# A routed-expert loop turned from two blocks per turn to one, with one set of rooms, in a hybrid decoder layer

## The chip, the cores and the metric

The kernel runs on one core of one Trainium2 chip. A core has TensorE (PE; its weight loads are listed apart as PEld), VectorE (DVE), ScalarE (ACT), GpSimd (POOL) and SyncE (SP), and 16 DMA engines that the queues of SP, ACT and POOL share. The metric is the device time of one execution in microseconds (us), of which the median of several runs is taken.

## The reference, cut to what matters

The program is one layer of a decoder trunk (2048 tokens, width 1024): a mixer (retention, Mamba-2 and S5 side by side), cross-attention, a hierarchical mixture of experts, and a last RMSNorm. The change touches the experts and the last norm only.

```python
def hier_moe(xn, w_rg, b_rg, w_re, b_re, w_gate, w_up, w_down):
    ...                                   # top-1 of 4 groups, then top-2 of its 8 experts
    flat_e = expert.reshape(-1)           # 4096 pairs (token, expert)
    counts = jnp.bincount(flat_e, length=N_EXPERTS)
    padded = (counts + MOE_BLOCK - 1) // MOE_BLOCK * MOE_BLOCK     # blocks of 128 rows
    ...
    def expert_block(args):
        xb, e = args
        h = jax.nn.silu(xb @ w_gate[e]) * (xb @ w_up[e])           # 1024 -> 512
        return h @ w_down[e]                                       # 512 -> 1024
    ...
    y = ybuf[dest].astype(F32) * sw[:, None]
    return jax.ops.segment_sum(y, st, num_segments=T).astype(xn.dtype)
```

Each expert's rows are filled up to whole blocks of 128. When the pairs that the reference routes on its own inputs are counted, all 32 experts get rows: 17 of them between 79 and 127 (one block each) and 15 between 133 and 203 (two blocks each). That makes 47 blocks, 6016 rows, of which 1920 are padding. In order of the experts the numbers of blocks are 2 1 1 2 2 2 2 2 1 2 2 1 2 1 1 2 1 1 1 2 1 1 2 2 1 1 2 1 1 1 2 1.

## The kernel before, in words

`experts` (line 2007) first routes on DVE with some help of PE, and writes a plan: for each block its expert, and whether it is the first block of its expert. Then all engines walk over the blocks. `finish` is the last norm.

**Number format.** Each f32 operand is split in two f16 halves, the nearest value and the rest, and a product is three f16 matmuls (`products`, line 110). So the weights of an expert (gate, up and down, 2 MB each) come in six pieces of 1 MB into six rooms `w_rows`; ACT takes the nearest (`nearest`, L2197), DVE the rest (`rest`, L2419), into one of two slots of `wg`, `wu` and `wd`, of which the current expert uses one and the next the other. A room is loaded again when DVE has taken its rest. The split of expert u+1 is tied to the first block b of expert u (`following`): gate and up pieces in step b, down pieces in step b+1.

**A step b** is, on PE: gate products of block b (24 matmuls), `turn_h(b-1)` (transposes of the hidden rows of b-1), `turn_x(b+1)` (transposes of the tokens of b+1, L2506), up products of b (24), down products of b-1 (24). ACT and DVE split the transposed tokens (`take_x`, L2224, and `x_rest`, L2437, into `xT`), apply silu (L2219) and product (L2432), split the hidden rows (`take_h`, `h_rest`), and ACT takes the result `y` out (`take_y`, L2234). Gate products of a block wait for its tokens and for the first two pieces of its expert; up products for the other two.

**Order of ACT and DVE in a step b.** ACT: down pieces (if any), silu(b), take_h(b-1), take_x(b+1), gate and up pieces (if any), take_y(b-1). DVE: down rests, h_rest(b-1), x_rest(b+1), gate and up rests, product(b).

**POOL** gathers the 128 token rows of a block from `xn_scr` into `xr` (L2143, an indirect DMA of 512 KB) and adds the 128 rows of `y` into `ybuf` (L2150, an indirect DMA that accumulates). Every room `xr`, `xT`, `sg`, `hT`, `y` is there twice, and a turn of the loop has two blocks, written out. So a gather waits for the transposes of two blocks earlier, and in POOL's list the adds stand two turns behind the gathers. The number of turns is rounded up: the loop runs 48 blocks, the last of them padding alone. Padding rows are moved like others: they gather row 2047, and they are added to 128 spare rows behind `ybuf`.

**finish** loads 16 chunks of 512 KB (SP), squares on ACT, mean on DVE, power on POOL, scaling on DVE, and stores each chunk (SP).

Of the kernel before, what the change touches and what calls it, by code (L numbers as in the profile page):

```python
# [17 lines left out]
F32 = mybir.dt.float32  # L18
F16 = mybir.dt.float16
I32 = mybir.dt.int32  # L20
U32 = mybir.dt.uint32
# [4 lines left out]
P = 128  # L26
# [1966 lines left out]
HB = 2  # L1993
# [3 lines left out]
MAX_TURNS = NB // HB - 1  # L1997
MIN_TURNS = (USED_MIN - 1) // HB

# [4 lines left out]
LISTED = 18  # L2004


def experts(nc, env, dram, logits, cst):
# [4 lines left out]
    with ExitStack() as ctx:  # L2012
# [18 lines left out]
        spare = [wd[:, 1, :, :, :].rearrange("p h k n -> p (h k n)").bitcast(F32), y[0][:, :], y[1][:, :]]  # L2031
# [29 lines left out]
        rows_from, rows_to = sb("rows_from", [P, NB], U32), sb("rows_to", [P, NB], U32)  # L2061
# [7 lines left out]
        x_ld = [sem(f"rows_gathered{i}") for i in range(HB)]  # L2069
# [3 lines left out]
        y_st = [sem(f"y_added{i}") for i in range(HB)]  # L2073
        NT = NB // HB
# [61 lines left out]
        @block.gpsimd  # L2136
        def _(pool):
            pool.wait_ge(rows_ok, 2)
# [6 lines left out]
            def add(b):  # L2145
# [4 lines left out]
                pool.indirect_dma_start(dram["ybuf"], bass.IndirectOffsetOnAxis(ap=rows_to[:, b:b + 1], axis=0), y[b % HB][:, :], None,  # L2150
                                        compute_op=ALU.add).then_inc(y_st[b % HB], 16)

            LATE = 2
            gather(0)
            gather(1)
            pool.wait_ge(planned, 1)
            used = turns_used(pool)
            for t in range(1, NT + LATE):
                if t < USED_MIN // HB:
                    gather(HB * t)  # L2160
                    gather(HB * t + 1)
                elif t < NT:
                    with pool.If(used + 1 > t):
                        gather(HB * t)
                        gather(HB * t + 1)
                if LATE <= t < USED_MIN // HB + LATE:
                    add(HB * (t - LATE))
                    add(HB * (t - LATE) + 1)
                elif t >= LATE:
                    with pool.If(used + 1 > t - LATE):  # L2170
                        add(HB * (t - LATE))
                        add(HB * (t - LATE) + 1)
            for i in range(HB):
                pool.wait_ge(y_st[i], used * 16 + 16)

        def steps(eng, first, step, last):
# [4 lines left out]
            with eng.Fori(0, MAX_TURNS) as t, eng.If(t < used):  # L2181
                step(t * HB + 1, 1, t)
                step(t * HB + 2, 0, t + 1)
            last(used * HB + 1, used)

        @block.scalar
        def _(act):
# [29 lines left out]
            def silu(b, i):  # L2217
                act.wait_ge(gd, b + 1)
                act.activation(sg[i][:, :], bank[2][:, :], ACT.Silu, scale=1.0 / (W_SCALE * X_SCALE)).then_inc(sil, 1)  # L2219

            def take_x(b, i):
# [470 lines left out]
```

## Time and profile before

| what | value |
|---|---|
| median of 3 runs (2547.68 to 2552.76) | 2551.65 us |
| the profiled execution itself | 2546.03 us |
| its span, first to last instruction | 2544.2 us |
| mean granted clock of PE | 0.959 |
| busy: PE, DVE, ACT, POOL | 2303.1, 1400.8, 983.4, 331.0 us |
| experts, first token transposes to last down product | 1633.1 to 2484.1 us |
| finish, first load to last landing | 2496.6 to 2544.2 us |

The span is cut in stages one after another. The mixer and cross-attention take the first 1590 us, routing some 40 us, the expert loop 850 us and `finish` 48 us. In a timeline a row is a run of equal instructions of one engine: start, length, engine, line, operation, output<-inputs, count, and in brackets the idle time before it with what ended that. Matmul rows overlap their successor by about 0.16 us, since the end of a matmul is modelled; the distance between two starts is the better measure.

### The profile page before, as it was taken

How to read it: one execution, taken by the hardware profiler on the slowest of the kernel's cores; microseconds unless marked ns; L12 is line 12 of the kernel's file. 1: busy time of each engine (PE TensorE's matmuls, PEld its weight loads, DVE VectorE, ACT ScalarE, POOL GpSimd, SP SyncE). 2: the span in 40 equal slices, each digit the busy share in tenths (PEclk: the TensorE clock that was granted, in tenths of full speed). 3: DMA queues.
4: the chain of work that ended last, by engine and by line, in shares of the span. 5: the costliest groups of instructions: out<-in, count | busy, mean ns of one | idle time of the engine just before them, and what ended most of it. 6: DMA issues, size and time to landing. Idle time of an engine off the chain costs nothing. (4 is left out here: it accounts for less than half of the span.)

```text
span 2544.2 us, 34574 instructions
## 1 busy us (share of the span) xinstructions
PE 2303.1 (91%) x12015; PEld 1304.5 (51%) x12016; DVE 1400.8 (55%) x2030; ACT 983.4 (39%) x1423; POOL 331.0 (13%) x275
## 2 busy tenths in 40 slices
PE   4999999999959988999999998489999999999980
PEld 2465565655648963555555554245545454444440
DVE  5566565565649843333333332867556578757823
ACT  4522533323221332222221221346545567646723
POOL 0022121210230000000000000012122221212112
PEclk8999999999979999999999999599999999999995
DMA  5201001001050142111111001579779899999927
GB/s 190 87 26 58 1 25 59 1 26 44 9 207 34 42 180 88 40 67 42 59 67 67 25 34 50 190 254 339 250 244 322 267 351 348 325 308 340 337 66 288
DMA packets 151077, 366.25 MB, mean 144 GB/s; under 512 B 24512, under 2 KB 30016, under 8 KB 150720
## 3 DMA queue, kind: packets, MB, share of 16 engines
q1 hardware_dynamic: 137152, 314.52, 33.8%
q0 software_dynamic: 13824, 50.34, 8.2%
q8 instruction: 69, 1.13, 0.2%
q14 instruction: 32, 0.26, 0.0%
HBM read 303.48 MB, written 61.34 MB: 143 GB/s over the span
## 5 line engine op out<-in xcount | busy, mean ns | idle before, releaser
L110 PE MATMUL bankA<-main_room,hnT 128*128 128x512 f16 (+1 forms) x1536 | 301.6, 354 | 5.5 <-DVE main_room L569 5.5
L110 PE MATMUL bankE<-wg,xT 128*128 128x512 f16 x1152 | 261.5, 384 | 20.9 <-DVE xT L2437 16.8
L110 PE MATMUL bankE<-wd,hT 128*128 128x512 f16 x1152 | 256.5, 379 | 1.7 <-DVE hT L2442 1.7
L110 PE MATMUL bankE<-wu,xT 128*128 128x512 f16 x1152 | 256.6, 379 | 0.0
L110 PEld LDWEIGHTS bankA<-main_room,hnT 128*128 128x128 f16 x1536 | 151.1, 99 | 147.7 <-issue 6.8
L110 PEld LDWEIGHTS bankE<-wg,xT 128*128 128x128 f16 x1152 | 113.8, 99 | 160.9 <-issue 28.8
L110 PEld LDWEIGHTS bankE<-wd,hT 128*128 128x128 f16 x1152 | 112.6, 98 | 137.6 <-issue 1.9
L110 PE MATMUL bankA<-hnT,main_room 128*128 128x512 f16 x768 | 174.2, 390 | 8.9 <-DVE hnT L545 8.9
L110 PEld LDWEIGHTS bankE<-wu,xT 128*128 128x128 f16 x1152 | 112.8, 98 | 125.5 <-issue 0.2
L110 PE MATMUL bankC<-w_probs,probsT 128*128 128x512 f16 x768 | 172.4, 382 | 0.0
L110 PE MATMUL bankC<-main_room,hnT_c 128*128 128x512 f16 x768 | 170.7, 379 | 0.0
L2419 DVE SCALAR_TENSOR_TENSOR wg<-w_rows,wg 128x2048 f16<-128x2048 f32 x64 | 143.9, 2287 | 31.7 <-ACT wg L2197 29.8
L2419 DVE SCALAR_TENSOR_TENSOR wd<-w_rows,wd 128x2048 f16<-128x2048 f32 x64 | 144.3, 2288 | 25.1 <-ACT wd L2197 25.0
L2419 DVE SCALAR_TENSOR_TENSOR wu<-w_rows,wu 128x2048 f16<-128x2048 f32 x64 | 144.3, 2286 | 14.1 <-ACT wu L2197 14.1
L2143 POOL DMA_INDIRECT xr<-scratch_xn_scr,rows_from x48 | 81.8, 1704 | 479.0 <-PE bankE L2506 435.4
L2197 ACT ACTIVATE wd<-w_rows 128x2048 f16<-128x2048 f32 x64 | 120.0, 1906 | 39.4 <-issue 24.5
L2442 DVE SCALAR_TENSOR_TENSOR hT<-bankE,hT 128x512 f16<-128x512 f32 x48 | 33.0, 687 | 184.0 <-ACT hT L2228 184.0
L110 PE MATMUL bankC<-w_out_s,catT 128*128 128x512 f16 x576 | 129.6, 379 | 1.4 <-DVE w_probs L1826 1.4
L2197 ACT ACTIVATE wu<-w_rows 128x2048 f16<-128x2048 f32 x64 | 119.5, 1899 | 26.1 <-DMA w_rows<-in_w_up 26.1
L110 PEld LDWEIGHTS bankA<-hnT,main_room 128*128 128x128 f16 x768 | 76.3, 100 | 103.9 <-issue 19.3
L2197 ACT ACTIVATE wg<-w_rows 128x2048 f16<-128x2048 f32 x64 | 119.1, 1904 | 25.8 <-issue 19.6
L1686 POOL TENSOR_TENSOR rs_c<-ms_c,nhalf_c 128x1 f32<-128x1 f32 x32 | 17.4, 543 | 827.2 <-DVE ms_c L1789 827.2
(365 smaller groups left out, 3389.6 us busy)
## 6 DMA issues: line engine op xcount, KB each, us to landing
w_rows<-in_w_gate SPq DMA_DIRECT2D x64, 1024.0 KB
w_rows<-in_w_up SPq DMA_DIRECT2D x64, 1024.0 KB
w_rows<-in_w_down SPq DMA_DIRECT2D x64, 1024.0 KB
x_room<-in_x SPq DMA_DIRECT2D x4, 2048.0 KB, 10.9
cat_t<-scratch_cat SPq DMA_DIRECT2D x16, 512.0 KB, 4.8
main_room<-in_x SPq DMA_DIRECT2D x16, 512.0 KB, 5.5
scratch_ybuf<-main_room SPq DMA_DIRECT2D x16, 512.0 KB, 2.6
hf<-scratch_ybuf SPq DMA_DIRECT2D x16, 512.0 KB, 12.0
```

What stands on the lines that cost most here:

```text
L110: ins = pe.matmul(o, a[x][k], b[y][k], start=start and k == 0 and j == 0, stop=stop and k == n - 1 and j == 2)
L1686: pool.tensor_tensor(rs[:, k, c:c + 1], ms[:, k, c:c + 1], nhalf[:, 0:1], ALU.pow).then_inc(rsd, 1)
L2143: pool.indirect_dma_start(xr[b % HB][:, :], None, dram["xn_scr"], bass.IndirectOffsetOnAxis(ap=rows_from[:, b:b + 1], axis=0)).then_inc(x_ ...
L2197: act.activation(place(p, slot, 0), room(p), ACT.Copy, scale=W_SCALE).then_inc(done, 1)
L2419: dve.scalar_tensor_tensor(place(p, slot, 1), room(p), W_SCALE, place(p, slot, 0), ALU.mult, ALU.subtract).then_inc(done, 1)
L2442: dve.scalar_tensor_tensor(hT[i][:, 1, :, :], bank[4][:, :].rearrange("p (k n) -> p k n", k=FT), H_SCALE, hT[i][:, 0, :, :], ALU.mult, ALU ...
```

## The change

- The loop has one block per turn and one room each of `xr`, `xT`, `sg`, `hT` and `y`. The number of turns is the number of blocks less two: 47 blocks are run.
- `turn_x(b+1)` on PE stands behind the up products of b.
- ACT: take_h(b-1), silu(b), down pieces, take_x(b+1), gate and up pieces, take_y(b-1). DVE: h_rest(b-1), down rests, product(b), x_rest(b+1), gate and up rests.
- POOL alternates: gather(b+1), which waits for the transposes of block b, then add(b-1), which waits for the add before it and for `y`. take_y(b) waits for the add of b-1 to have landed. The last block's add uses a list of its own, `rows_end`.
- Gather and add carry a bound of T-1 on the row number, and rows beyond it (the padding) are left out. `xr` is cleared once by DVE at the start of routing.
- Before the loop, DVE takes x_rest(1) ahead of the gate and up rests of expert 1.
- `finish` issues its even chunk loads on SP and its odd ones on ACT.

```diff
-MAX_TURNS = NB // HB - 1
-MIN_TURNS = (USED_MIN - 1) // HB
+MAX_TURNS = NB - 3
+MIN_TURNS = USED_MIN - 2
...
-        xr = [sb(f"xr{i}", [P, D]) for i in range(HB)]
-        xT = [sb(f"xT{i}", [P, 2, KT, P], F16) for i in range(HB)]
-        sg = [sb(f"sg{i}", [P, DE]) for i in range(HB)]
-        hT = [sb(f"hT{i}", [P, 2, FT, P], F16) for i in range(HB)]
-        y = [sb(f"y{i}", [P, D]) for i in range(HB)]
+        xr, xT = sb("xr", [P, D]), sb("xT", [P, 2, KT, P], F16)
+        sg, hT, y = sb("sg", [P, DE]), sb("hT", [P, 2, FT, P], F16), sb("y", [P, D])
...
             def gather(b):
-                if b >= HB:
-                    pool.wait_ge(xt, 2 * (b - HB) + 2)
-                pool.indirect_dma_start(xr[b % HB][:, :], None, dram["xn_scr"], bass.IndirectOffsetOnAxis(ap=rows_from[:, b:b + 1], axis=0)).then_inc(x_ld[b % HB], 16)
...
                 if b:
-                    pool.wait_ge(y_st[(b - 1) % HB], (b - 1) // HB * 16 + 16)
+                    pool.wait_ge(xt, 2 * b)
+                pool.indirect_dma_start(xr[:, :], None, dram["xn_scr"], bass.IndirectOffsetOnAxis(ap=rows_from[:, b:b + 1], axis=0),
+                                        bounds_check=T - 1, oob_is_err=False).then_inc(x_ld, 16)
+
+            def add(b, rows):
+
+                if b:
+                    pool.wait_ge(y_st, b * 16)
                 pool.wait_ge(y_t, b * 2 + 2)
...
+            def turn(b):
+                gather(b + 1)
+                add(b - 1, rows_to[:, b - 1:b])
...
         @block.scalar
...
-            def step(b, i, k):
+            def step(b):
+                take_h(b - 1)
+                silu(b)
                 following(act, b - 1, downs_(b - 1))
-                silu(b, i)
-                take_h(b - 1, 1 - i)
-                take_x(b + 1, 1 - i)
+                take_x(b + 1)
                 following(act, b, gates_ups(b))
-                take_y(b - 1, 1 - i, k if i else k - 1)
+                take_y(b - 1)
...
         @block.vector
...
+            dve.memset(xr[:, :], 0.0).then_inc(x_clear, 1)
...
             def first():
...
-                product(0, 0)
+                product(0)
+                x_rest(1)
                 gate_up_rest(1, 1)
-                x_rest(1, 1)
...
-            def step(b, i, k):
+            def step(b):
+                h_rest(b - 1)
                 following(dve, b - 1, down_rest)
-                h_rest(b - 1, 1 - i)
-                x_rest(b + 1, 1 - i)
+                product(b)
+                x_rest(b + 1)
                 following(dve, b, gate_up_rest)
-                product(b, i)
...
         @block.tensor
...
-            def step(b, i, k):
-                def turns():
-                    turn_h(b - 1, 1 - i)
-                    turn_x(b + 1, 1 - i, k + 1 if i else k)
-
-                by_slot(b, gate_up(b, i, turns))
-                by_slot(b - 1, down(b - 1, 1 - i))
+            def step(b):
+                by_slot(b, gate_up(b, lambda: turn_h(b - 1)))
+                turn_x(b + 1)
+                by_slot(b - 1, down(b - 1))
...
         @block.scalar
         def _(act):
+            for c in range(1, NCH, 2):
+                act.dma_start(H[c][:, :], hv[c]).then_inc(h_ld[c], 16)
```

PE, one step of the loop as it stood before: `wg`, `wu` and `wd` are gate, up and down weights, `cst_all,xr` the token transposes, `cst_all,sg` those of the hidden rows.

```order
L110 MATMUL bankE<-wg,xT 128x512 x24
L2514 MATMUL bankE<-cst_all,sg 128x128 x4
L2500 ISA
L2501 ISA
L2506 MATMUL bankE<-cst_all,xr 128x128 x8
L2538 REGISTER_ALU
L110 MATMUL bankE<-wu,xT 128x512 x24
...
L110 MATMUL bankE<-wd,hT 128x512 x24
```

The same step now.

```order
L110 MATMUL bankE<-wg,xT 128x512 x24
L2514 MATMUL bankE<-cst_all,sg 128x128 x4
L2538 REGISTER_ALU
L110 MATMUL bankE<-wu,xT 128x512 x24
...
L2500 ISA
L2501 REGISTER_ALU
L2506 MATMUL bankE<-cst_all,xr 128x128 x8
...
L110 MATMUL bankE<-wd,hT 128x512 x24
```

The token transposes moved from ahead of the up products to behind them; between them and the next gate products only the down products stand.

POOL, from the first gathers into the loop, before.

```order
L2143 DMA xr<-scratch_xn_scr,rows_from 128x1024 x2
L2079 TENSOR_LOAD plan
L2079 ISA x2
L2143 DMA xr<-scratch_xn_scr,rows_from 128x1024 x4
L2150 DMA scratch_ybuf<-y,rows_to 2176x1024 x2
L2143 DMA xr<-scratch_xn_scr,rows_from 128x1024 x2
```

And now.

```order
L2141 DMA xr<-scratch_xn_scr,rows_from 128x1024 x2
L2076 TENSOR_LOAD plan
L2076 ISA x2
L2141 DMA xr<-scratch_xn_scr,rows_from 128x1024
L2149 DMA scratch_ybuf<-y,rows_to 2176x1024
L2141 DMA xr<-scratch_xn_scr,rows_from 128x1024
```

Six gathers stood ahead of the first add; now three do, and the add of block b-2 stands directly ahead of the gather of block b+1.

## Rows read from the trace of the kernel before

**Rows 1.** Page, part 1: busy us (share of the span) and instructions.

```profile
PE 2303.1 (91%) x12015; PEld 1304.5 (51%) x12016; DVE 1400.8 (55%) x2030; ACT 983.4 (39%) x1423; POOL 331.0 (13%) x275
```

**Rows 2.** Windows of the loop: busy us (instructions), then clock, DMA share, GB/s.

```profile
core 0: us, PE busy (x) PEld busy (x) DVE busy (x) ACT busy (x) POOL busy (x), PEclk, DMA share, GB/s
1680.00:2450.00 770.00, 762.43 (x3790) 379.05 (x3789) 516.33 (x361) 472.25 (x450) 154.25 (x88) 1.00 0.89 297
```

**Rows 3.** Page, part 5: the gate matmuls; idle before them and its releaser.

```profile
L110 PE MATMUL bankE<-wg,xT 128*128 128x512 f16 x1152 | 261.5, 384 | 20.9 <-DVE xT L2437 16.8
```

**Rows 4.** Timeline, PE, from the token transposes in the step of a one-block expert.

```profile
2062.55 1.04 PE L2506 MATMUL bankE<-cst_all,xr 128*128 128x128 f32 x8
2063.42 5.34 PE L110 MATMUL bankE<-wu,xT 128*128 128x512 f16 x24
2068.60 5.34 PE L110 MATMUL bankE<-wd,hT 128*128 128x512 f16 x24
```

**Rows 5.** Timeline, DVE, same step: rests of tokens, then of gate weights.

```profile
2065.41 1.28 DVE L2437 SCALAR_TENSOR_TENSOR xT<-bankE,xT 128x512 f16<-128x512 f32 x2
2067.23 4.50 DVE L2419 SCALAR_TENSOR_TENSOR wg<-w_rows,wg 128x2048 f16<-128x2048 f32 x2 [0.53 <-issue]
```

**Rows 6.** Timeline, ACT: take_x of that step; gate pieces and take_y in another.

```profile
2063.29 1.09 ACT L2224 ACTIVATE xT<-bankE 128x512 f16<-128x512 f32 x2
...
2098.73 3.71 ACT L2197 ACTIVATE wg<-w_rows 128x2048 f16<-128x2048 f32 x2 [0.65 <-issue]
...
2105.95 0.57 ACT L2234 ACTIVATE y<-bankE 128x512 f32<-128x512 f32 x1
2107.68 0.60 ACT L2234 ACTIVATE y<-bankE 128x512 f32<-128x512 f32 x1 [1.16 <-PE bankE L110]
```

**Rows 7.** Timeline, POOL: the add that follows that take_y.

```profile
2109.05 1.98 POOL L2150 DMA_INDIRECT scratch_ybuf<-y,rows_to  x1 [8.60 <-ACT y L2234]
```

**Rows 8.** One line's instructions (ns min/median/max): gathers of the loop, one of them, adds.

```profile
L2143 POOL DMA_INDIRECT xr<-scratch_xn_scr,rows_from x43: 939/1879/2650, 1693.2 to 2408.1; - x43
...
DMA to landing us min/median/max: 4.1/8.4/10.1
...
L2143 POOL DMA_INDIRECT xr<-scratch_xn_scr,rows_from x1: 1522/1522/1522, 2080.7 to 2080.7; - x1
...
DMA to landing us min/median/max: 7.9/7.9/7.9
...
L2150 POOL DMA_INDIRECT scratch_ybuf<-y,rows_to x42: 1582/1616/2621, 1694.4 to 2386.2; - x42
...
DMA to landing us min/median/max: 6.0/9.5/11.3
```

**Rows 9.** Timeline, PE: four instructions behind an idle stretch of PE.

```profile
2166.30 1.12 PE L2514 MATMUL bankE<-cst_all,sg 128*128 128x128 f32 x4 [2.93 <-DVE sg L2432]
2167.21 1.91 PE L2506 MATMUL bankE<-cst_all,xr 128*128 128x128 f32 x8
...
2425.92 0.66 PE L2514 MATMUL bankE<-cst_all,sg 128*128 128x128 f32 x4 [2.51 <-DVE sg L2432]
...
2458.82 7.03 PE L110 MATMUL bankE<-wg,xT 128*128 128x512 f16 x24 [4.15 <-issue]
```

**Rows 10.** Waits of PE, 1680 us to the end: total us, times, longest.

```profile
PE bankE L2514 <- DVE sg L2432: 7.5, 4, 2.9
```

**Rows 11.** Timeline, start of the loop: product(0), x_rest(1), gate products of block 1.

```profile
1656.97 0.75 DVE L2432 SCALAR_TENSOR_TENSOR sg<-bankE,gate_of,sg 128x512 f32<-128x512 f32 x1
...
1666.45 1.28 DVE L2437 SCALAR_TENSOR_TENSOR xT<-bankE,xT 128x512 f16<-128x512 f32 x2
...
1668.08 6.65 PE L110 MATMUL bankE<-wg,xT 128*128 128x512 f16 x24 [12.57 <-DVE xT L2437]
```

**Rows 12.** Timeline, DVE: a clearing of 512 columns at the start of routing.

```profile
1593.48 0.48 DVE L2268 MEMSET wd<- 128x512 f32 x1 [0.46 <-PEq L1565]
```

**Rows 13.** Windows of finish, columns as in rows 2.

```profile
2522.00:2532.00 10.00, 0.00 (x0) 0.00 (x0) 7.99 (x12) 2.90 (x6) 5.58 (x5) 0.50 1.03 419
```

More of the change, by code:

```diff
@@ L1992 @@
 WHOLE = 12582912.0
-HB = 2
 SLOTS = 2
@@ L2068, in experts @@
         hi_gu, lo_gu, hi_dn, lo_dn = sem("gate_up_nearest"), sem("gate_up_rest"), sem("down_nearest"), sem("down_rest")
-        x_ld = [sem(f"rows_gathered{i}") for i in range(HB)]
+        x_ld = sem("rows_gathered")
         lists, marked, listed, rows_ok = sem("list_steps"), sem("pairs_marked"), sem("rows_listed"), sem("rows_known")
@@ L2072, in experts @@
             "xT_done", "xT_nearest", "xT_rest", "gate_done", "up_done", "silu_done_e", "h_ready", "hT_done", "hT_nearest", "hT_rest", "down_done", "y_taken"))
-        y_st = [sem(f"y_added{i}") for i in range(HB)]
-        NT = NB // HB
+        y_st, y_end, end_st = sem("y_added"), sem("last_y_taken"), sem("last_y_added")
+        x_clear = sem("rows_cleared")
         block = ctx.enter_context(nc.Block())
@@ L2157, in _ @@
             used = turns_used(pool)
[L2158 to L2174, printed above, removed]
+            def turn(b):
+                gather(b + 1)
+                add(b - 1, rows_to[:, b - 1:b])
+            for b in range(1, MAX_TURNS + 2):
+                if b < USED_MIN:
+                    turn(b)
+                else:
+                    with pool.If(used + 2 > b):
+                        turn(b)
+            pool.wait_ge(lists, LISTED)
+            pool.wait_ge(y_end, 2)
+            pool.indirect_dma_start(dram["ybuf"], bass.IndirectOffsetOnAxis(ap=rows_end[:, :], axis=0), y[:, :], None,
+                                    bounds_check=T - 1, oob_is_err=False, compute_op=ALU.add).then_inc(end_st, 16)
+            pool.wait_ge(end_st, 16)
+            pool.wait_ge(x_ld, used * 16 + 48)
         def steps(eng, first, step, last):
@@ L2181, in steps @@
             with eng.Fori(0, MAX_TURNS) as t, eng.If(t < used):
-                step(t * HB + 1, 1, t)
-                step(t * HB + 2, 0, t + 1)
-            last(used * HB + 1, used)
+                step(t + 1)
+            last(used + 1)
         @block.scalar
@@ L2238, in first, with last @@
                     nearest(p, 0, 0)
-                take_x(0, 0)
-                silu(0, 0)
+                take_x(0)
+                silu(0)
                 for p in GU:
                     nearest(p, 1, 1)
-                take_x(1, 1)
-            def step(b, i, k):
+                take_x(1)
+            def step(b):
+                take_h(b - 1)
+                silu(b)
                 following(act, b - 1, downs_(b - 1))
-                silu(b, i)
-                take_h(b - 1, 1 - i)
-                take_x(b + 1, 1 - i)
+                take_x(b + 1)
                 following(act, b, gates_ups(b))
-                take_y(b - 1, 1 - i, k if i else k - 1)
-            def last(b, k):
+                take_y(b - 1)
+            def last(b):
+                take_h(b - 1)
+                silu(b)
                 following(act, b - 1, downs_(b - 1))
-                silu(b, 1)
-                take_h(b - 1, 0)
-                take_y(b - 1, 0, k)
-                take_h(b, 1)
-                take_y(b, 1, k)
+                take_y(b - 1)
+                take_h(b)
+                take_y(b, y_end)
             steps(act, first, step, last)
@@ L2446, in first @@
                     rest(p, 0, 0)
-                x_rest(0, 0)
+                x_rest(0)
                 for p in GU[2:]:
@@ L2528, in rows @@
                         return [[w[:, slot, h, kt, :] for kt in range(KT)] for h in range(2)]
-                    tokens = [[xT[i][:, h, kt, :] for kt in range(KT)] for h in range(2)]
+                    tokens = [[xT[:, h, kt, :] for kt in range(KT)] for h in range(2)]
                     pe.wait_ge(x_hi, b * 2 + 2)
@@ L2541, in gate_up, with down @@
                 return products_of
-            def down(b, i):
+            def down(b):
                 def products_of(slot, u):
@@ L2596, in _ @@
         def _(sp):
-            hv = dram["ybuf"][0:T, :].rearrange("(c p) d -> c p d", p=P)
             ov = dram["out"][0].rearrange("(c p) d -> c p d", p=P)
-            for c in range(NCH):
+            for c in range(0, NCH, 2):
                 sp.dma_start(H[c][:, :], hv[c]).then_inc(h_ld[c], 16)
```

95 lines of the change are left out of this document (49 added, 46 removed).

## The prediction

> **What bounds the kernel now.** I read the busy shares first, then windows of the loop, then timelines of single steps. PE is busy for 91% of the span [rows 1], and in the loop for 762.4 of 770 us at full clock [rows 2]: nothing but PE sets the pace there, although the DMA engines are 89% busy beside it. So a step costs what its PE work costs. By the starts in [rows 4] that is 0.87 us for the token transposes (2062.55 to 2063.42) and 5.18 us for 24 products (2063.42 to 2068.60), three times in a step; the four hidden transposes take half of the eight, 0.43. The step is 0.87 + 0.43 + 3 x 5.18 = 16.84 us. Of the gate products' 20.9 us of idle time 16.8 are waits for split tokens, all ahead of the loop [rows 3]. The question is thus not what engines save, but whether PE still finds its operands ready.
>
> **What the change takes away.**
> (a) Block 48. The blocks of the reference are 47, and 48 are run (1152 gate matmuls [rows 3] / 24). One step less: -16.8 us. Its weights are those of the last expert, so no load goes with it.
> (b) Block 1's tokens. x_rest(1) began at 1666.45, behind four gate and up rests, though product(0) had ended at 1657.7 [rows 11]. Now it follows product(0): 8.7 us earlier, and PE has nothing else to wait for: -8.7 us. The rests behind it then end where x_rest(1) used to, in time for block 2.
> (c) In four steps PE waited 7.5 us in all for product(b) [rows 10], which stood behind rests of late weights. It now stands ahead of the rests. I take -5.
> (d) Routing: clearing 1024 columns is twice the 0.48 us of [rows 12], and four small steps ahead of the gate list less two steps of the turn count add some 0.4: +1.4 us.
> (e) Padding rows: 1920 of 6016 are not moved. Where PE is the bound, this is worth nothing by itself; it can only shorten the waits below.
> (f) finish: in its middle the DMA engines run at a share of 1.03 and 419 GB/s [rows 13]. Its 17 MB in and out set its length, and a second issuing queue moves no byte faster: 0, between -2 (an earlier start of the first loads) and +4 (eight issues on ACT ahead of its first square).
> Together -29 us.
>
> **What it adds: a wait for weights.** I count from the start of turn_x. Tokens must be turned, split, and then, where block b is the only one of its expert, the gate pieces of the next expert must be split before PE can begin gate(b+1). In [rows 4, 5] this chain took from 2062.55 to 2067.23 + 4.50 = 2071.73, that is 9.18 us, and hid below up and down products (11.2 us with the transposes). The chain keeps its order on ACT and DVE; product(b) is slipped in while take_x runs and costs nothing. But turn_x now has only the down products behind it: 0.87 + 5.18 = 6.05 us of cover. PE waits 9.18 - 6.05 = 3.13 us. If the expert before had one block too, two down rests (4.5) stand ahead on DVE in the same step: hidden transposes end 5.6 us into the step, take_h, silu and the plan's loads bring the first down piece to 7.2, its nearest takes 1.9 (3.71 for two, [rows 6]), two rests end at 13.6, product and x_rest at 15.6, and with 0.5 of issue and 4.5 the gate rests at 20.6: 3.75 us late against 16.84. Of the 17 one-block experts 16 have a successor, 8 of them behind another one-block expert: 8 x 3.13 + 8 x 3.75 = **+55 us**. In a two-block expert's second step, x_rest ends at 15.6 by the same count, 1.2 before it is due, and nothing waits.
>
> **What it adds: a wait for the gather.** gather(b+1) used to be two blocks ahead; the adds behind it could be late. Now it stands behind add(b-2), which stands behind take_y(b-2), which stands behind the four pieces on ACT in a step b-1 that splits. From the start of gate(b-1): turn_x starts at 10.8; take_x ends 1.83 later (2062.55 to 2064.38, [rows 4, 6]), 12.6; the plan 0.7; four pieces 7.2 (2098.73 to 2105.95, [rows 6]), 20.5; take_y 1.1, 21.6; add after 0.8 (2108.28 to 2109.05, [rows 6, 7]), its 1.6 to 2.0 us of issue [rows 7, 8] and a gap of 0.3: the gather starts at 24.4. PE wants the rows for turn_x(b+1) at 16.84 + 10.8 = 27.6. With L from issue to landing it waits L - 3.2. L was 4.1 to 10.1, median 8.4 [rows 8]; none of these gathers had to hurry. What the trace doesn't show is a gather directly behind an add, with four weight loads just issued. The floor is 4.1, the ceiling 10.1. I take 7.9, the row of 2080.7 [rows 8], a gather issued while weight loads were still draining as here: 4.7 us, for 14 two-block experts (the first one's split lies ahead of the loop): +65 us (floor 13, ceiling 97). For one-block experts PE is 3.1 to 3.75 late already and the wait is L - 6.6, 1.3 us; a slower clock (next) delays the need as well, so I count half, 0.6 x 16 = +10 (floor 0, ceiling 50). **+75 us** in all.
> The landing of one gather is also priced by the Trainium skill ("DMA: Bandwidth & Descriptors", section "Anatomy of one DMA — SWDGE (gpsimd) path"): about 2.0 us + bytes / 436e3, which for 512 KB is 3.2 us. By it no two-block step would wait, and the sum would be 65 us less. [Rows 8] disagree: 4.1 at best, 8.4 in the median, beside weight loads.
> The skill also says, against this change, to double-buffer so that DMA overlaps compute ("Trainium Kernel Development and Optimization", section "Best Practices"); the trace of before has only the doubled rooms.
>
> **What it adds: clock.** Behind an idle stretch of 2.93 us the hidden and token transposes took 1.12 and 1.91 us, against 0.66 behind one of 2.51 us [rows 9] and 1.04 in the loop [rows 4]: they ran at the lower level of the clock, some 1.3 us lost. Behind 4.15 us, 24 products took 7.03 [rows 9] against 5.34 [rows 4]: 1.7 lost. The 30 waits above are 3.1 to 4.7 us long, on this edge. Between 0 and 1.7 each; I take 1.0: **+30 us**.
>
> **Sum.** Against the profiled execution's own 2546.0 us (span 2544.2 and 1.8 around it): 2546 - 29 + 55 + 75 + 30 = 2677. The timed median stands 5.6 us above that execution. I forecast **2678 us**, about 5% more.
>
> **Rivals.**
> *The gather comes at its unloaded speed* (L = 4.1). For it: missing padding rows and longer steps relieve the DMA engines. Against: four loads of 1 MB are issued 17 to 24 us into the very step. Then 55 + 13 + clock on 16 waits, 16: 2546 - 29 + 84 = 2601.
> *The gather waits for the add's rows* (L = 10.1 or more, clock lost at every wait). For it: both go through one queue, and adds need 9.5 us in the median [rows 8]. 2546 - 29 + 55 + 97 + 38 + 50 = 2757.
> *Not slower.* The waits for weights don't come, because the gate rests are done within the 6.05 us behind turn_x; then only (a) to (d) remain, 2517. This needs rests that start 1.5 us after turn_x does; in [rows 4, 5] they started after 4.7. It decides at 3.1 us per step, and I see no row for it.
> *The turn count isn't what it says.* If 48 blocks still ran, each case is 17 us longer. The count of the reference speaks against it.
>
> **Chances.** Forecast 0.68 (its own range 2630 to 2725), unloaded gather 0.16, queued gather 0.11, not slower 0.04, the last 0.01. The range 2608 to 2742 leaves about 2 in 10 outside. A measurement tells about 0.2% (5 us) from no change: faster 0.04, same 0.01, slower 0.95.
>
> **What would show each step.** In the changed profile: 1128 gate matmuls; the gate products' idle time near 55 us in 16 or so waits of 3 to 4 us for DVE `wg`; the token transposes idle near 75 us for the DMA of `xr`; gate products of block 1 at about 1660; PE near 85% busy in the loop; transposes of 1.1 or products of 7 us behind some waits; finish still 48 us long. Wrong it would be if PE's wait for `xr` were near zero or above 100 us, which is the choice of L, or if one-block steps took 16.8 us.

## The result: 9% slower, 1.75 times what was forecast

The changed kernel takes 2772.6 us (median of 4 runs, 2770.6 to 2774.8), the kernel before 2550.7 beside it: a ratio of 1.087, 95% interval 1.085 to 1.089, or +222 us. The forecast was 2678 us, +127; its own sum of terms is +131. The direction was as forecast, and so were the two kinds of wait; the size was not, the empty turns of the loop were missing from the sum, and the time lies outside the range.

The profiled execution has a span of 2773.0 us against 2544.2. Page, part 1, of the changed kernel, and its window of the loop (columns as in [rows 2]):

```profile
PE 2360.8 (85%) x11931; PEld 1318.9 (48%) x11932; DVE 1405.2 (51%) x2029; ACT 986.1 (36%) x1417; POOL 334.7 (12%) x274
```

```profile
1680.00:2450.00 770.00, 632.61 (x2874) 304.34 (x2872) 389.50 (x271) 358.29 (x338) 124.04 (x68) 0.90 0.65 214
```

PE, busy for 762.4 of these 770 us before [rows 2], is now busy for 632.6, at a mean clock of 0.90, and the DMA engines' share fell from 0.89 to 0.65. They are less loaded and yet they are what PE waits for. The waits of PE from 1600 us to the end of the changed kernel (what PE waited for, then total us, times, longest):

```profile
PE bankE L2506 <- DMA xr<-scratch_xn_scr,rows_from: 139.4, 31, 9.0
PE bankE L110 <- DVE wg L2419: 37.5, 16, 3.0
...
PE bankE L110 <- issue: 14.3, 10, 10.2
...
PE bankE L110 <- DVE wd L2419: 1.3, 4, 0.6
```

Page, part 5, the groups of PE that take these waits (the first answers to [rows 3]):

```profile
L110 PE MATMUL bankE<-wg,xT 128*128 128x512 f16 x1128 | 274.1, 403 | 54.7 <-DVE wg L2419 37.5
...
L110 PE MATMUL bankE<-wd,hT 128*128 128x512 f16 x1128 | 283.2, 413 | 7.1 <-issue 4.1
...
L2506 PE MATMUL bankE<-cst_all,xr 128*128 128x128 f32 x376 | 64.8, 330 | 139.4 <-DMA xr<-scratch_xn_scr,rows_from 139.4
```

The instructions behind waits also ran longer. Timeline of PE in the changed kernel, three places where transposes or gate products waited:

```profile
1701.59 5.35 PE L110 MATMUL bankE<-wg,xT 128*128 128x512 f16 x24 [2.99 <-DVE wg L2419]
...
2005.86 1.94 PE L2506 MATMUL bankE<-cst_all,xr 128*128 128x128 f32 x8 [9.00 <-DMA xr<-scratch_xn_scr,rows_from]
2007.60 6.94 PE L110 MATMUL bankE<-wd,hT 128*128 128x512 f16 x24
...
2092.89 1.06 PE L2506 MATMUL bankE<-cst_all,xr 128*128 128x128 f32 x8 [1.33 <-DMA xr<-scratch_xn_scr,rows_from]
2094.49 5.35 PE L110 MATMUL bankE<-wd,hT 128*128 128x512 f16 x24 [0.54 <-issue]
```

Behind 1.33 us of idleness nothing is lost, nor behind the 2.99 at 1701.59. Behind 9.00 us the transposes take 1.94 us, not 1.04, and the down products 6.94, not 5.34 [rows 4]: 2.5 us on top of the wait. The mean granted clock from 2006 to 2012 us is 0.60 of full speed, so part of that stretch ran at the lower level, 1.2 GHz.

The loop's own balance, from the start of block 1's gate products to the end of the last down products: 816.0 us before (1668.08 to 2484.08), 1051.4 now (1663.47 to 2714.86), although there is one step less. What stands in the 228.8 us by which the spans differ:

| where | us |
|---|---|
| one step less (counted, 16.84 us of work) | -16.8 |
| block 1's gate products, counted from the first token transposes | -8.8 |
| waits for the product (7.5 us before, none now) | -7.5 |
| finish, 47.6 to 45.3 us | -2.3 |
| first token transposes at 1637.35, not 1633.13; 2.4 of it arose ahead of routing | +4.2 |
| waits for `xr` in the loop, two-block experts' second steps (14 waits) | +93.3 |
| the same in the other steps (16 waits) | +45.2 |
| waits for `wg` | +37.5 |
| waits with no releaser in the profile, 14.3 against 4.15 [rows 9] | +10.1 |
| waits for the rests of `wd` | +1.3 |
| slow clock: gate, down and transpose groups longer than before per instruction, 18.1 + 32.1 + 14.3 | +64.5 |
| left over; 47 waits, each seen 0.16 us too short by the modelled ends of matmuls, would be 7.5 | +8.1 |

### The profile page after: what moved, and what is told of

It is laid out like the page before. It is cut to its first block and busy times, and to the rows that moved or that the text cites. A ratio compares the mean times of both kernels' runs of the same rounds, so it can differ in the third digit from the quotient of the medians.

```text
span 2773.0 us, 34998 instructions
## 1 busy us (share of the span) xinstructions
PE 2360.8 (85%) x11931; PEld 1318.9 (48%) x11932; DVE 1405.2 (51%) x2029; ACT 986.1 (36%) x1417; POOL 334.7 (12%) x274
## 5 line engine op out<-in xcount | busy, mean ns | idle before, releaser
L110 PE MATMUL bankE<-wg,xT 128*128 128x512 f16 x1128 | 274.1, 403 | 54.7 <-DVE wg L2419 37.5
L110 PE MATMUL bankE<-wd,hT 128*128 128x512 f16 x1128 | 283.2, 413 | 7.1 <-issue 4.1
L2149 POOL DMA_INDIRECT scratch_ybuf<-y,rows_to x46 | 119.2, 2590 | 869.4 <-ACT y L2231 829.1
L2506 PE MATMUL bankE<-cst_all,xr 128*128 128x128 f32 x376 | 64.8, 330 | 139.4 <-DMA xr<-scratch_xn_scr,rows_from 139.4
L2419 DVE SCALAR_TENSOR_TENSOR wd<-w_rows,wd 128x2048 f16<-128x2048 f32 x64 | 143.8, 2288 | 65.6 <-ACT wd L2194 65.5
L2419 DVE SCALAR_TENSOR_TENSOR wg<-w_rows,wg 128x2048 f16<-128x2048 f32 x64 | 143.8, 2288 | 55.6 <-ACT wg L2194 55.6
L2419 DVE SCALAR_TENSOR_TENSOR wu<-w_rows,wu 128x2048 f16<-128x2048 f32 x64 | 143.6, 2285 | 0.0
L2221 ACT ACTIVATE xT<-bankE 128x512 f16<-128x512 f32 x94 | 53.1, 596 | 249.6 <-PE bankE L2506 249.6
L2194 ACT ACTIVATE wg<-w_rows 128x2048 f16<-128x2048 f32 x64 | 118.9, 1904 | 26.8 <-issue 26.6
L2506 PEld LDWEIGHTS bankE<-cst_all,xr 128*128 128x128 f32 x376 | 53.8, 171 | 156.4 <-issue 152.4
## 6 DMA issues: line engine op xcount, KB each, us to landing
w_rows<-in_w_up SPq DMA_DIRECT2D x64, 1024.0 KB, 10.4
```

The lines of the kernel that those rows point to most:

```text
L110: ins = pe.matmul(o, a[x][k], b[y][k], start=start and k == 0 and j == 0, stop=stop and k == n - 1 and j == 2)
L2194: act.activation(place(p, slot, 0), room(p), ACT.Copy, scale=W_SCALE).then_inc(done, 1)
L2221: act.activation(xT[:, 0, 4 * j:4 * j + 4, :], bank[j][:, :].rearrange("p (k n) -> p k n", k=4), ACT.Copy, scale=X_SCALE).then_inc(x_hi, 1)
L2419: dve.scalar_tensor_tensor(place(p, slot, 1), room(p), W_SCALE, place(p, slot, 0), ALU.mult, ALU.subtract).then_inc(done, 1)
L2506: ins = pe.transpose(bank[j][:, n * P:(n + 1) * P], xr[:, kt * P:(kt + 1) * P], ident[:, :])
```

## The experiments

Seven of them change the changed kernel (e...), seven the kernel before (b...). All times are medians; where a kernel ran more than once, a ratio to the kernel before with its 95% interval is given. `...` marks lines left out of an edit.

**e1: the place of the gather in POOL's list.** The changed kernel, with the gather of b+1 ahead of the add of b-2.

```diff
-                gather(b + 1)
-                add(b - 1, rows_to[:, b - 1:b])
...
+                gather(b + 1)
+                if b > 1:
+                    add(b - 2, rows_to[:, b - 2:b - 1])
```

> The changed kernel with one thing moved in POOL's list: gather(b+1) stands ahead of add(b-2) instead of behind it. Rooms, order on PE, ACT and DVE, and padding stay. Theory A (the place in the list is what makes the gather late; one room is enough): the gather is issued right behind the transposes of block b, some 16 us before its rows are wanted, and even at 9 us to landing it is in time. PE's wait for xr (139.4 us in the changed kernel) falls under 10, the slow-clock stretches behind it go too (some 45 us), and the time falls from 2773 to about 2590. Rival B (the one room itself is what costs): the wait stays above 60 us, since the room is free only after the transposes of the block before, and the time stays above 2680.

Measured: 2578.2 us (one run), 194 us less. Its waits of PE:

```profile
PE bankE L110 <- DVE wg L2420: 49.0, 16, 3.4
...
PE bankE L2507 <- DMA xr<-scratch_xn_scr,rows_from: 0.9, 1, 0.9
```

The waits for `xr` in the loop are gone (the 0.9 us lie ahead of it), and with them most of the slow clock: the groups of PE are 11.7 us longer than before, not 64.5. The one room is kept. The room is not what costs; the add ahead of the gather is. The gather could start when the transposes have emptied `xr`, but it stands behind an add that stands behind take_y. The one room `y` has a wait too, since take_y needs the add before it to have landed (ACT waits 48.0 us for that here, in 13 places), but no wait of PE follows from it in this profile. Timeline of POOL in the changed kernel, and behind it in this one:

```profile
1774.60 1.59 POOL L2149 DMA_INDIRECT scratch_ybuf<-y,rows_to  x1 [18.17 <-ACT y L2231]
1776.49 1.04 POOL L2141 DMA_INDIRECT xr<-scratch_xn_scr,rows_from  x1 [0.30 <-issue]
1795.36 3.16 POOL L2149 DMA_INDIRECT scratch_ybuf<-y,rows_to  x1 [17.83 <-ACT y L2231]
1798.83 1.04 POOL L2141 DMA_INDIRECT xr<-scratch_xn_scr,rows_from  x1 [0.30 <-issue]
```

```profile
1732.48 2.13 POOL L2141 DMA_INDIRECT xr<-scratch_xn_scr,rows_from  x1 [11.74 <-PE bankE L2507]
1742.54 3.27 POOL L2149 DMA_INDIRECT scratch_ybuf<-y,rows_to  x1 [7.94 <-ACT y L2232]
```

**e2, e3, e7: what makes the landing slow.** In the changed kernel the adds lose all rows but row 0 (e2: bound 0 instead of T-1), the loop's weight loads bring a quarter of their bytes (e3), or both (e7). All three leave out work that the result needs, and are read for their time alone.

```diff
-                                        bounds_check=T - 1, oob_is_err=False, compute_op=ALU.add).then_inc(y_st, 16)
+                                        bounds_check=0, oob_is_err=False, compute_op=ALU.add).then_inc(y_st, 16)
...
+                    a = a // 2
+                    sp.dma_start(room(p)[:, 0:a, 0:256], rows[e].squeeze(0)[:, k:k + a, 0:256]).then_inc(w_ld[p], 16)
```

> The changed kernel, but the adds in the loop carry a bound of 0 on the row number, so that they leave out all rows but row 0: this leaves the experts' part out of the result, and the time is read for that. The adds stand where they stood and are issued as before. Theory C (the gather lands late because the add's 128 rows are ahead of it in the same queue): issue to landing of the gather, 7.9 us in the median and near 9 behind the four weight pieces, falls to 4 to 5, PE's wait for xr falls from 139 to 50 us or less, time about 2660. Rival D (weight loads in flight make it late): landing stays at 8 to 9 and the wait above 110 us; time within 20 us of 2773.

> The changed kernel, but in the loop each weight load brings a quarter of its bytes (half the rows of the piece, half the columns), the rest of the room stays what the first loads left; the result is wrong for that, and all splits and products run as before. Rival D: with a quarter of the weight traffic the gather behind an add lands in 4 to 6 us, and PE's wait for xr falls from 139 to about 60 us; time about 2670. Theory C: the add is still ahead of the gather, landing stays above 7.5 and the wait above 100 us.

> The changed kernel with both aids at once: the adds find no row within their bound (the experts' part of the output is left out) and the loop's weight loads bring a quarter of the bytes (later experts use stale weights). One alone took 43 and 77 us from the 139 us of waits for xr. If what is left is the gather's own late issue behind the add, it still waits where the landing takes longer than the 1.8 to 3.2 us that it has: a landing of 4.1 us, the fastest of the kernel before, would leave 14 to 31 waits of 1 to 2 us, 15 to 50 us in all, and about 2640 to 2670 us. If rows and loads were the whole cause, the waits are 0 to 19 us (139 less 43 less 77), and the time 2600 to 2640.

Measured: 2712.7, 2689.5 and 2653.8 us (one run each). The waits of PE for `xr`, in e2, e3 and e7 in turn:

```profile
PE bankE L2506 <- DMA xr<-scratch_xn_scr,rows_from: 97.6, 29, 6.4
```

```profile
PE bankE L2510 <- DMA xr<-scratch_xn_scr,rows_from: 62.3, 17, 6.2
```

```profile
PE bankE L2510 <- DMA xr<-scratch_xn_scr,rows_from: 46.4, 15, 5.3
```

The median from issue to landing of a gather was 7.9 us in the changed kernel, 6.6 in e2, 5.5 in e3 and, in e7 (DMA issues of its window from 1600 us on):

```profile
xr<-scratch_xn_scr,rows_from POOLq DMA_INDIRECT x48, 4.3
```

Taking away the adds' rows alone takes 42 us off the waits, the weight loads alone 77, both together 93. Neither is the whole cause, and for the adds' rows I had expected about twice as much. The last 46 us, 2.5 to 5.3 in each of 13 two-block experts and some 1 at two other places, are there although the landing has little left to contend with, a quarter of the weight bytes: that is the late issue itself. It is the rival of the unloaded gather (L = 4.1) with the issue where it really was.

**e4: the padding rows, in the changed kernel.** Bounds are taken off gather and add, so that padding is moved as in the kernel before.

```diff
-                                        bounds_check=T - 1, oob_is_err=False).then_inc(x_ld, 16)
...
-                                        bounds_check=T - 1, oob_is_err=False, compute_op=ALU.add).then_inc(y_st, 16)
+                                        compute_op=ALU.add).then_inc(y_st, 16)
```

> The changed kernel with its padding rows moved again as before (no bound on the row numbers; padding gathers row 2047 and is added behind the result). If leaving out padding shortened gathers and adds, this is slower: by theory C by 10 to 40 us, since the blocks before a late gather are often half empty and their add is short; if each of the 16 DMA engines has full lists either way, or landing is set by weight loads (rival D), it is the same within 10 us.

Measured: 2805.1 us (one run), 32 more; waits for `xr` 166.0 instead of 139.4 us, gathers landing after 9.5 us in the median instead of 7.9. Leaving padding out is worth 32 us here, 26.6 of them in these waits: a landing is what PE waits for here.

**b5: the padding rows, in the kernel before.** The same bounds, and both rooms `xr` cleared at the start of routing.

```diff
+            for room_x in xr:
+                dve.memset(room_x[:, :], 0.0).then_inc(x_clear, 1)
...
+                                        bounds_check=T - 1, oob_is_err=False).then_inc(x_ld[b % HB], 16)
```

> The kernel before with one edit: gathers and adds leave padding rows out (and both token rooms are cleared at the start of routing, 2 us of DVE). In the changed kernel leaving them out was worth 32 us, 26 of them in waits for a late gather. Here a gather is two blocks ahead and no wait for it is in the trace; if the saving lives only by that wait, it is 0 here, with a further -0 to -7 from the waits for a late product that stands behind late weights, and +2 for the clearing: 2549 us, between 2544 and 2553. If freed DMA time were worth something in itself, the time would be well below 2544.

Measured: 2542.2 us, ratio 0.9965 (0.9953 to 0.9977): -9.5 us, more of a gain than I expected. Its trace shows two places. Waits for the product are 2.9 us in one, against 7.5 in four [rows 10]. And the last block, which is padding alone, adds nothing: from the issue of the last add to the first load of finish it takes 8.0 us (2488.97 to 2496.98), before 11.1 (2485.46 to 2496.60). These are 7.7 us; the clearing costs some 2 of them back. PE's waits for the first tokens' rests are 15.4 us instead of 16.8, and I have no row for the rest.

**e5: the gate pieces ahead of the tokens.** e1, and on ACT and DVE the two gate pieces of the next expert are split ahead of take_x and x_rest, so that gate(b+1) would not wait for them. The part on DVE, against e1:

```diff
-                product(b)
+                following(dve, b, gate_rest)
+                product(b)
                 x_rest(b + 1)
-                following(dve, b, gate_up_rest)
+                following(dve, b, up_rest)
```

> e1_gather_first with the split of the gate pieces moved ahead of the tokens on ACT and DVE (the up pieces stay behind them). Theory E (the 49 us that PE still waits for the rest of wg are the chain turn_x, take_x, gate pieces behind the up products): where the expert before had two blocks, the gate rests now end 13.6 us into the step and x_rest at 15.6, in time for 16.84, so 8 of the 16 waits vanish. Where it had one, DVE has two down rests and two gate rests first (to 18.3) and x_rest ends near 20: 3.5 us of wait for xT instead of wg, 8 times. Sum: waits 49 to about 28 us, time 2578 to about 2540. Rival F (the wait is set by DVE's sum of work, whatever its order): waits stay at 49, time within 10 us of 2578.

Measured: 2615.9 us, ratio 1.026 (1.024 to 1.028): not 38 us faster than e1 but 38 slower. The wait changed its name. Timeline of DVE, and of PE, in e5:

```profile
1725.93 4.50 DVE L2426 SCALAR_TENSOR_TENSOR wd<-w_rows,wd 128x2048 f16<-128x2048 f32 x2 [2.19 <-ACT wd L2195]
1730.34 4.49 DVE L2426 SCALAR_TENSOR_TENSOR wg<-w_rows,wg 128x2048 f16<-128x2048 f32 x2
1734.74 0.75 DVE L2447 SCALAR_TENSOR_TENSOR sg<-bankE,gate_of,sg 128x512 f32<-128x512 f32 x1
1735.40 1.28 DVE L2452 SCALAR_TENSOR_TENSOR xT<-bankE,xT 128x512 f16<-128x512 f32 x2
```

```profile
1737.03 8.25 PE L110 MATMUL bankE<-wg,xT 128*128 128x512 f16 x24 [3.42 <-DVE xT L2452]
```

PE now waits for `xT`, 73.1 us in 32 places from 1600 us on, where e1 waits 49.0 for `wg`; 7.0 us in two of these places lie ahead of the loop and are in e1 too. The other half of the loss is the clock: the gate products take 287.0 us in all, in e1 268.6. This place had no wait in e1: its step is the first of a two-block expert, where the gate pieces aren't urgent and the tokens are. An order written once for all steps moves a wait from the steps that need the one to those that need the other.

**e6, b6: the empty turns.** The loop had a fixed number of turns and an `If` around each; here it has only those that are used, in e1 (e6) and in the kernel before (b6).

```diff
-            with eng.Fori(0, MAX_TURNS) as t, eng.If(t < used):
+            with eng.Fori(0, used) as t:
```

> e1_gather_first with a loop that runs as many turns as there are, instead of 61 of which the last 16 do nothing. Theory G (PE's 10.2 us idle ahead of the last block's gate products, 4.2 in the kernel before with 8 empty turns of 31, are the empty turns, 0.5 to 0.7 us each): the wait shrinks to 1 us or less and the time falls by 9 to 11 us, to about 2568. Rival H (it is the loading of the code of the last step): the wait stays near 10 and the time at 2578.

> The kernel before with a loop of as many turns as there are, instead of 31 of which the last 8 do nothing. Theory G: PE's wait of 4.2 us ahead of block 48 and the 1.7 us of slow clock behind it vanish, time 2550.5 falls by 4 to 6 us. Rival H: no change (within 2 us).

Measured: e6 2567.8 us, ratio 1.0072 (1.0054 to 1.009), 10.4 less than the one run of e1; b6 2544.1 us, ratio 0.9974 (0.9964 to 0.9984), 6.9 less than before, a little more than the 4 to 6 expected. The wait ahead of the last block's gate products, 10.24 us in the changed kernel and 4.15 before [rows 9], is gone in both. In the changed kernel, and in e6:

```profile
2689.16 7.46 PE L110 MATMUL bankE<-wg,xT 128*128 128x512 f16 x24 [10.24 <-issue]
```

```profile
2486.53 5.34 PE L110 MATMUL bankE<-wg,xT 128*128 128x512 f16 x24
```

The kernel before has 31 turns at most and uses 23, the changed one 61 and 45. So 8 empty turns cost 4.15 us and 16 cost 10.24, 0.52 and 0.64 each, and then the clock. The rival, the loading of the last step's code, falls with that: the code is the same and the wait is gone.

**b1, b2: two of the parts alone, in the kernel before.** x_rest(1) ahead of the gate and up rests; and 47 blocks, with a last step written out for an odd number. The edit of b1, and the heart of that of b2:

```diff
                 product(0, 0)
+                x_rest(1, 1)
                 gate_up_rest(1, 1)
-                x_rest(1, 1)
```

```diff
-            last(used * HB + 1, used)
+            odd = odd_count(eng)
+            with eng.If(odd > 0):
...
+                step(less * HB + 1, 1, less)
+                last(less * HB + 2, 0, less + 1)
+            with eng.If(odd < 1):
+                last(used * HB + 1, 1, used)
```

> The kernel before with one edit: DVE takes the rests of block 1's tokens ahead of the gate and up rests of expert 1. By the count from the rows the gate products of block 1 start 8.7 us earlier and everything behind them too: 2542.0 us, between 2540 and 2544. A rival: the rests of gate and up weights end 2.5 us later and with them the first product of the loop, so that block 2 waits and part of the gain is given back, 2545 or more.

> The kernel before, with 47 blocks run instead of 48: two blocks per turn and two sets of rooms as before, and behind the loop one step more and an ending of the other parity where the number of blocks is odd. Nothing else is changed. Theory I (a block is 16.84 us of PE work and nothing hides it): time 2550.5 falls by 15 to 18 us, to about 2534. Rival: the end of the loop is set by the adds or the code of the ending, and the gain is under 8 us.

Measured: b1 2543.4 us, ratio 0.9969 (0.9958 to 0.9979), -8.4; b2 2536.6 us, ratio 0.9942 (0.9926 to 0.9959), -14.5, just under the 15 to 18 expected. In b2 the written-out step brings one wait of its own:

```profile
PE bankE L110 <- DVE wu L2434: 5.8, 1, 5.8
```

**b8, b9: the late token transposes alone.** The kernel before, with two rooms, and turn_x behind the up products (b8); in b9 DVE also takes the product ahead of the tokens' rests.

```diff
-                    turn_h(b - 1, 1 - i)
-                    turn_x(b + 1, 1 - i, k + 1 if i else k)
-
-                by_slot(b, gate_up(b, i, turns))
+                by_slot(b, gate_up(b, i, lambda: turn_h(b - 1, 1 - i)))
+                turn_x(b + 1, 1 - i, k + 1 if i else k)
...
+                product(b, i)
                 x_rest(b + 1, 1 - i)
                 following(dve, b, gate_up_rest)
-                product(b, i)
```

> The kernel before, with two rooms and two blocks per turn, and one edit: the token transposes stand behind the up products, as in the changed kernel. The rows of tokens are two blocks ahead, so nothing of the gather's price can appear; what does is the price of the shorter cover alone. If the wait for weights belongs to the place of the transposes on PE and to nothing else, the waits for wg are those of the changed kernel with its gather put right, 49 us in 16 waits, and the slow clock behind them costs what is left there, 8 us: 2550.7 + 57 = 2608 us, between 2598 and 2618. If the one room or the one-block turn had a part in that wait, it is well below 49 us here and the time nearer to 2575. The rival of the prediction by which the rests are done in time would give 2551.

> The kernel before with late token transposes (as in b8_turns_late) and one more edit: DVE takes the product ahead of the tokens' rests, as in the changed kernel. If the 31 us of added waits for the product and the slow clock behind them in b8_turns_late come from that place in DVE's order, both go, the waits for wg stay near 46 us, and the time falls from 2665.5 to about 2608 us (2600 to 2616). If they come from the two rooms or the pair of blocks, it stays near 2665.

Measured: b8 2665.5 us, ratio 1.045 (1.044 to 1.047), 58 above what I expected; b9 2621.2 us (2610.8 to 2626.5), ratio 1.028 (1.026 to 1.031). Waits of PE in b8, then in b9:

```profile
PE bankE L110 <- DVE wg L2419: 46.1, 16, 3.0
PE bankE L2514 <- DVE sg L2432: 38.7, 14, 2.9
```

```profile
PE bankE L110 <- DVE wg L2419: 46.1, 16, 3.0
...
PE bankE L110 <- DVE hT L2442: 12.2, 14, 1.7
```

The wait for weights, 46.1 us, is the place of turn_x: b8 has two rooms and two blocks per turn. (e1 has 49.0; for these 2.9 us more I have no run.) What b8 adds is a wait for the product. Timeline of DVE in b8:

```profile
1743.69 1.29 DVE L2437 SCALAR_TENSOR_TENSOR xT<-bankE,xT 128x512 f16<-128x512 f32 x2 [3.50 <-ACT xT L2224]
1747.10 4.49 DVE L2419 SCALAR_TENSOR_TENSOR wg<-w_rows,wg 128x2048 f16<-128x2048 f32 x2 [2.12 <-ACT wg L2197]
1751.51 4.48 DVE L2419 SCALAR_TENSOR_TENSOR wu<-w_rows,wu 128x2048 f16<-128x2048 f32 x2
1755.91 0.74 DVE L2432 SCALAR_TENSOR_TENSOR sg<-bankE,gate_of,sg 128x512 f32<-128x512 f32 x1
```

Later tokens make the rests later, and the product stands behind them. The miss of 58 us is this wait (31.2 us more than before) and the clock behind it: gate and up products and the hidden transposes take 33.7 us more than before. With the product ahead, 38.7 us become 10.5 for the hidden rows (12.2 less the 1.7 that stood before), and 44 us of time go. b9 came out 10 us above its profiled execution in the median, and 5 above the interval that I had given.

**b7: the parts that cost nothing, together.** The kernel before with two rooms and its own order, 47 blocks, block 1's tokens early, padding left out, the final loads on two queues, and no empty turns; the edits are those of b1, b2, b5 and b6.

```diff
-            for c in range(NCH):
+            for c in range(0, NCH, 2):
...
+            for c in range(1, NCH, 2):
+                act.dma_start(H[c][:, :], hv[c]).then_inc(h_ld[c], 16)
```

> The kernel before with two rooms and its order of PE, and all of the change's parts that cost nothing there: 47 blocks, block 1's tokens early, padding rows left out, final loads on two queues, and a loop that counts only the turns that are used. The sum of the single measurements and counts: 2550.7 - 14.5 (47 blocks) - 8.7 (tokens) - 6.9 (turns) - 2.3 (final loads) = 2518.3, with padding between +2 and -7 and some 2 us of it already counted twice where the odd ending waits for late up weights: 2517 us, between 2510 and 2522. If the parts get into each other's way (a loop without empty turns and a written-out odd ending both lie at the loop's end, where code is fetched), it is 2525 or more.

Measured: 2512.6 us (2511.7 to 2515.0), ratio 0.9854 (0.9839 to 0.9869): 39 us faster than the kernel before and 260 faster than the changed one. Its loop window shows PE as the bound again:

```profile
1680.00:2450.00 770.00, 766.50 (x3816) 380.69 (x3815) 515.17 (x360) 472.99 (x452) 144.30 (x88) 1.00 0.83 282
```

## Why the prediction was wrong, point by point

- **(a) to (d) and (f)** held, or nearly: block 48 is 16.8 us of steps by the count (-14.5 when taken away alone, b2), block 1's tokens 8.8 (8.4 alone, b1), the waits for the product 7.5 instead of 5, routing 1.8 instead of 1.4 (the 2.4 ahead of it aside), finish -2.3, just beyond the near end of what I gave, -2.
- **The wait for weights, +55.** Right in place (16 waits, none elsewhere) and a little high in size: 37.5 us, and 46 to 49 where the gather doesn't disturb (e1, b8, b9). The 2.99 us at 1701.59 stand against 3.13; behind another one-block expert 3.4 in e1 against 3.75. In the changed kernel the down products that cover the chain are often slow, 6.9 us instead of 5.3, and so cover more.
- **The wait for the gather, +75: the term that failed most**, with 138.5. The count of the list was right up to the add: in the splitting step that starts at 1772.95 it is issued after 22.4 us, as forecast, and PE wants the rows after 27.65. The step that failed is the price behind it: two durations were too short. I gave the add 1.6 to 2.0 us of issue, and it took 3.16, held up by VectorE (last section): the gather began after 25.9 us, not 24.4. In 13 of the 14 two-block steps PE wanted the rows 1.7 to 4.3 us after the gather's start, 2.6 in the mean, where I had 3.2. And I took L = 7.9; in these 13 steps it was 7.5 to 10.9, 9.4 in the mean. That is the larger error. With some 0.2 us from landing to start they waited 7.0 us each, not 4.7; the last, behind which no weights are loaded, had L = 5.8 and waited 1.8. Together 93.3 instead of 65. The row of 2080.7 was no bad likeness in kind (an add had been issued at 2077.25, 3.5 us ahead), but a single one.
- **The same wait in the other 16 steps.** I had written L - 6.6 and halved it, 10 us in all; it was 45.2, 2.8 each: L was 8.6 in the mean, PE wanted the rows 6.0 after the gather's start, and the slow clock did not delay the need as the halving supposed.
- **What L is made of** e2, e3 and e7 show: 4.3 us in the median with the adds' rows and three quarters of the weight bytes away. The rival of the queued gather, 2757 us at a chance of 0.11, was nearest to the truth. Its reason is only a part of it: the adds' rows make 42 of the 139 us, the weight loads 77. (Its sum has 38 us for the one-block steps, for which the term's own ceiling is 50, and by L - 6.6 in 16 steps 56.)
- **(e), padding worth nothing by itself**, was too little: 32 us in the changed kernel, where it shortens the waits as (e) allowed for without a figure (e4), and 9.5 in the kernel before (b5), where PE is the bound and where I had written off the last block of padding alone and its add at the very end.
- **The clock, +30.** The mechanism was there and the size off: 64.5 us. Behind the 16 waits for weights the gate products ran 18.1 us longer, 1.1 each, close to the 1.0 that I took. Behind the 30 waits for rows it was 46.4, 1.5 each, since they were longer than I thought, up to 9.0 us and then 2.5 lost. The term hung on the one before it; an error there was paid twice.
- **Not in the sum at all:** the empty turns. I counted the turns of the plan, not those of the loop; twice as many turns are 16 empty ones instead of 8, +6.1 us and some clock. I had the row, 4.15 us of "issue" ahead of the last block [rows 9], and used it for the clock alone. The 4.1 us beside it are nine waits of some 0.5 us.

Too low were thus the gather by 63.5, the clock by 34.5, the empty turns and other small waits by 11.4, and the waits' unseen ends by 8; too high the weights by 17.5. That is 100 us; routing and what lies ahead of it add 2.8, and the product and finish take 4.8 back: 98, which is the miss by the spans (228.8 against the sum's 131). The forecast's last step left out 5 us more: its sum, 2677 us, is for the profiled execution, and the timed median, which it says stands 5.6 us above that, would have been 2683.

## What to carry to other kernels

When a room is given up, look at what the refill stands behind in its queue's list, not at the room: with one room and the gather first, nothing in the loop waited for rows (2578 us), and with the add first the same program took 2773. Price a wait by the instruction that holds it up, issue time under load included, and let a term that depends on a wait (clock, contention) grow with it in the range. And of a change with many parts, those that shorten a list of known waits (b7, -39 us) can be had without the one that turns the list around.

## What the runs showed of the hardware

- **The issue of a gather or an add is held up while VectorE takes the rest of a weight piece, until that ends.** Of the 44 adds of the changed kernel from 1700 to 2700 us, 14 began while no such instruction (L2419) ran, and their issue took 1.59 us. The other 30 took 2.21 to 3.17, all but two of them 3.16 or 3.17, and each ended 1.45 to 1.47 us behind the end of the rest that was running. The row of 1795.36 above is one of them: VectorE's second piece ran until 1797.06, and the add ended at 1798.52. Where the two lie otherwise, the length is another and the distance stays. At 2545.99 the rest ended after 0.74 us, and the issue took 2.21. Timeline of DVE at the first place, and of DVE and POOL at the second:

```profile
1792.57 4.49 DVE L2419 SCALAR_TENSOR_TENSOR wu<-w_rows,wu 128x2048 f16<-128x2048 f32 x2
...
2542.24 4.49 DVE L2419 SCALAR_TENSOR_TENSOR wu<-w_rows,wu 128x2048 f16<-128x2048 f32 x2
2545.99 2.21 POOL L2149 DMA_INDIRECT scratch_ybuf<-y,rows_to  x1 [20.32 <-issue]
```

  In the kernel before, 29 gathers of the loop began beside a rest and ended 0.83 to 0.89 us behind its end, after 1.18 to 2.65 us; the 14 others took 0.94 to 1.00. Token rests (L2437), of which one input lies in PSUM, held up nothing: in e1 the gather at 1766.17 took 1.04 us although one (there L2438) ran from 1765.64 to 1766.93. The Trainium skill ("SBUF — State Buffer", section "SBUF: two separate sides") says that VectorE and GpSimd share one pair of ports as an exclusive lock, which a VectorE instruction in a two-port mode, or one with two SBUF inputs against a GpSimd instruction that reads SBUF, keeps for its whole length. The rows agree: a weight rest has both inputs in SBUF, and the issue waits until it is done. That it is the port, and not something else that the two share, no run here shows.
- **The landing of a gather of up to 128 rows (512 KB)** has no fixed price: with padding left out 4.3 us in the median with light loads and empty adds (e7), 5.5 with light loads (e3), 6.6 with empty adds (e2), 7.9 with both as they are, and 9.5 with padding moved too (e4).
- **The same idle stretch can cost nothing or 1.7 us of slow clock.** Behind 2.99 us 24 gate products took 5.35 us at 1701.59, and behind the same 2.99 us 7.04 at 2078.91; in e1, behind 3.36 us, they took 8.11 at 1717.11, at a mean granted clock of 0.65.
